# The experts' stage: VectorE makes all parts of the low weights, GpSimd only moves rows

## The reference, cut to what matters

```
for e in range(16):
    hid = silu(xt @ exp_w1[e]) * (xt @ exp_w3[e])        # 1024 -> 256, twice
    y   = y + gate[:, e:e+1] * (hid @ exp_w2[e])         # 256 -> 1024
```

## Time and profile before

| | us |
|---|---|
| median of 3 runs (lowest to highest) | 1619.41 (1618.01 to 1620.03) |
| the profiled execution | 1620.24 |
| its span in the profile | 1618.5 |
| experts: first up_lo on VectorE to the last y_ps matmul | 1126.6 to 1550.3 |
| TensorE busy in the span | 1449.3 (90%) |
| VectorE busy in the span | 1125.9 (70%) |
| GpSimd busy in the span | 483.4 (30%) |

### The profile page before, as it was taken

One profiled execution on the slowest core, in us unless ns is written; L12 is line 12 of the kernel. 1 busy time (PEld: TensorE's weight loads), 2 busy tenths in 40 slices (PEclk: granted clock), 3 DMA queues, 4 the chain that ended last, 5 costly groups with the idle time before them and its releaser, 6 DMA issues. The chain is left out here.

```text
span 1618.5 us, 30220 instructions
## 1 busy us (share of the span) xinstructions
PE 1449.3 (90%) x8946; PEld 1261.0 (78%) x8947; DVE 1125.9 (70%) x2208; ACT 927.7 (57%) x1625; POOL 483.4 (30%) x345
## 2 busy tenths in 40 slices
PE   5999989999976899999999999973999999999940
PEld 5999977777754899999999999972777788777820
DVE  8787548999955888888888888877444333444237
ACT  3444338787855766666666666632555544556325
POOL 1212124575520011111121111122454534544218
PEclk9999999999988999999999999995899999999975
DMA  8865542534444112211112221126798787796576
GB/s 286 303 226 200 211 145 86 189 144 173 165 147 138 61 39 93 72 65 59 59 60 80 76 78 59 47 97 198 233 270 263 182 248 207 200 273 164 104 224 257
DMA packets 126214, 250.09 MB, mean 155 GB/s; under 512 B 24498, under 2 KB 77746, under 8 KB 126132
## 3 DMA queue, kind: packets, MB, share of 16 engines
q1 hardware_dynamic: 94000, 160.97, 28.7%
q0 software_dynamic: 12528, 45.99, 12.3%
q10 hardware_dynamic: 19604, 42.09, 6.8%
HBM read 154.35 MB, written 94.67 MB: 154 GB/s over the span
## 5 line engine op out<-in xcount | busy, mean ns | idle before, releaser
L1736 DVE TENSOR_TENSOR d_probs_t_lo<-d_pt_ps,d_probs_t_hi 128x512 fp32r<-128x512 f32 x256 | 164.9, 686 | 63.4 <-ACT d_probs_t_hi L1650 61.8
L1914 POOL TENSOR_TENSOR d_h_tile<-d_s_tile,d_ln_g_b 128x512 f32<-128x512 f32 x30 | 38.9, 1296 | 532.3 <-ACT d_s_tile L1683 514.6
L1650 ACT ACTIVATE d_probs_t_hi<-d_pt_ps 128x512 fp32r<-128x512 f32 x256 | 139.2, 596 | 95.9 <-PE d_pt_ps L1531 89.5
L1712 DVE TENSOR_REDUCE d_neg_max<-d_s_ps 128x1 f32<-128x1024 f32 x128 | 155.6, 1215 | 3.5 <-PE d_s_ps L1520 3.5
L121 PE MATMUL acc<-k_hi,wl_hi 128*128 128x256 f32 x512 | 145.2, 284 | 4.5 <-DVE k_lo L576 4.5
L121 PE MATMUL e_a_ps<-up_hi,e_xt_hi 128*128 x336 | 136.6, 406 | 10.8 <-issue 5.5
L1633 ACT ACTIVATE d_probs<-d_s_ps,d_neg_max 128x1024 f32<-128x1024 f32 x128 | 143.5, 1121 | 4.2 <-DVE d_neg_max L1712 4.2
L122 PE MATMUL acc<-k_lo,wl_hi 128*128 128x256 f32 x512 | 144.3, 282 | 0.0
L123 PE MATMUL acc<-k_hi,wl_lo 128*128 128x256 f32 x512 | 144.3, 282 | 0.0
L1531 PE MATMUL d_pt_ps<-ident,d_probs 128*128 128x128 f32 x1024 | 132.9, 273 | 4.7 <-ACT d_probs L1633 3.2
L1545 PE MATMUL d_ot_ps<-d_probs_t_hi,d_v_split 128*128 128x256 f32 x512 | 127.4, 287 | 8.3 <-DVE d_probs_t_lo L1736 8.3
(11 more groups left out here) (405 smaller groups left out, 4079.2 us busy)
## 6 DMA issues: line engine op xcount, KB each, us to landing
up_raw<-in_exp_w SPq DMA_DIRECT2D x32, 1024.0 KB, 13.0
down_raw<-in_exp_w SPq DMA_DIRECT2D x16, 1024.0 KB, 13.0
d_h_tile<-h_dram SPq DMA_DIRECT2D x16, 522.0 KB, 4.7
h_dram<-v_all ACTq DMA_DIRECT2D x16, 512.0 KB
ht_hi_dram<-k_hi ACTq DMA_DIRECT2D x8, 1024.0 KB, 4.3
ht_lo_dram<-k_lo ACTq DMA_DIRECT2D x8, 1024.0 KB, 6.7
q_dram<-wq_raw ACTq DMA_DIRECT2D x16, 512.0 KB, 3.0
d_q_tile<-q_dram SPq DMA_DIRECT2D x16, 512.0 KB, 4.2
```

The lines of the kernel that those rows point to most:

```text
L1650: act.activation(pt_hi[:, c * HALF:(c + 1) * HALF, h % 2], pt_ps[c][:], ACT.Copy).then_inc(pth_done[c], 1)
L1712: dve.tensor_reduce(nm[:, u, h:h + 1], s_ps[h % 2][:], AX, ALU.max, negate=True).then_inc(nm_done, 1)
L1736: dve.tensor_tensor(pt_lo[:, part, h % 2], pt_ps[c][:], pt_hi[:, part, h % 2].bitcast(F32), ALU.subtract)\
L1914: pool.tensor_tensor(h1[:, part], s_t[u][:, part], g_b[:, part], ALU.mult).then_inc(hg_done, 1)
```

## The change

GpSimd makes no low weights any more. VectorE makes all four up parts in `split_first` and both down parts in `split_rest`. The two semaphores of GpSimd go, and every consumer waits for four up parts and two down parts of VectorE alone. The same holds before the first tile. Buffers, matmuls, transfers and ScalarE's work are as they were.

```diff
-        UP_POOL = 3
-        DOWN_POOL = 1
...
-        up_lo_pool = sem("up_lo_made_by_pool")
-        down_lo_pool = sem("down_lo_made_by_pool")
...
-        up_lo_parts = ((up_lo_made, UP_PARTS - 1), (up_lo_pool, 1))
-        down_lo_parts = ((down_lo_made, DOWN_PARTS - 1), (down_lo_pool, 1))
+        up_lo_parts = ((up_lo_made, UP_PARTS),)
+        down_lo_parts = ((down_lo_made, DOWN_PARTS),)
...
         def _(pool):
...
-            def split_rest(e):
-                make_up_lo(pool, e, UP_POOL, up_lo_pool)
-                make_down_lo(pool, e, DOWN_POOL, down_lo_pool)
...
-            split_rest(0)
-            last = run_tiles(pool, skip, ahead, None, skip, skip, down, skip, split_rest)
+            last = run_tiles(pool, skip, ahead, None, skip, skip, down, skip, None)
...
         def _(dve):
...
             def split_first(e):
                 for i in range(UP_PARTS):
-                    if i != UP_POOL:
-                        make_up_lo(dve, e, i, up_lo_made)
+                    make_up_lo(dve, e, i, up_lo_made)
 
             def split_rest(e):
                 for k in range(DOWN_PARTS):
-                    if k != DOWN_POOL:
-                        make_down_lo(dve, e, k, down_lo_made)
+                    make_down_lo(dve, e, k, down_lo_made)
```

## The result

The changed kernel takes 1644.71 us (median of 4 runs, 1638.77 to 1647.53) against 1619.72 us for the kernel before (4 runs beside them, 1618.01 to 1623.37). The ratio is 1.0129, 95% interval 1.0106 to 1.0152: slower, by 17 to 25 us (the two medians alone lie 25.0 us apart, at the top of that). The forecast was 1634.8 us, in a range of 1628 to 1643. By the ratio, 1.0129 x 1619.41 = 1640.3 us, the result lies near the upper end of that range; the median itself lies above it. The direction and the main term were right, and some 8 us are missing.

A forecast was written before the change was run, and what follows sets the result against it. TensorE sets the pace and loses time in split tiles, where `hid` stands behind VectorE's up parts. 16.0 - 0.3 - 0.3 = +15.4 us gave 1634.8 us on the runs' median, range 1628 to 1643.

The forecast's parts named there:

- the main term: In 14 split tiles, a fourth VectorE up part makes `hid` and TensorE 1.14 us later each: 16.0 us.
- The fourth up part: In split tiles, one more subtraction ahead of `hid` delays TensorE 1.14 us in each of 14 tiles: 16.0 us.
- The distance behind hid: Between the end of `hid` and the next tile, what TensorE does doesn't change; 1.27, 2.15 or 2.56 us.
- Weight loads and scatters: Earlier loads delay scatters before seven split tiles, 0 to +8.4 us; longer experts gain 0 to -4; both taken as 0.
- The second down part: In plain tiles, VectorE's second down part ends before `hid` is due, with over 1 us slack behind it: 0 us.
- GpSimd's leaving: TensorE's wait for GpSimd before tile 4 goes, -0.3 us; tile 4's high parts wait less for SP, -0.3 us.
- Tile 0 and the rest: Extra subtractions before tile 0 are hidden and its block's earlier start covers 1.14 us: 0 us; stages outside experts don't move.
- signs of being wrong: Wrong if `hid` idles before it in split tiles, plain tiles grow, split blocks start elsewhere, or stages outside experts move.
- late scatters: Rival, 10%: before seven split tiles each `gate` is the whole 1.2 us late, 8.4 us more, 1643 us.
- GpSimd is what TensorE waits for: Rival, 3%: each change of expert hangs on GpSimd's up part; 0.6 us won at 14 changes, 1611 us.
- nothing moves: Rival, 4%: `hid` late by 1.14 us is absorbed somewhere behind TensorE's matmuls, 1619 us.

The follow-up runs named there:

- repeat1: Kernel before, with VectorE repeating one up subtraction into an unread spare buffer behind its three up parts, ahead of `hid`; ratio 1.0124 to the kernel before.
- up_only: Changed kernel without its second half: VectorE makes all four up parts, GpSimd keeps down part 1; ratio 1.0123 to the kernel before.
- gate_late: Kernel before, with VectorE copying `gate` and scatter indices of the previous tile right behind `hid` of the next; 1616.70 us, ratio 0.9956 to the kernel before.
- change_gate_late: Changed kernel, with VectorE copying `gate` and scatter indices of the previous tile behind `hid` of the next; 1629.48 us, ratio 1.0038 to the kernel before.
- repeat2: Kernel before, with VectorE repeating one up subtraction twice into unread spare buffers ahead of `hid` in split tiles; ratio 1.0321 to the kernel before.
- down_wait: down_only, but GpSimd begins its up part only when VectorE's two down parts are done; ratio 1.0002 to the kernel before.
- down_only: Changed kernel without its first half: VectorE makes both down parts, GpSimd keeps up part 3; ratio 1.0089 to the kernel before.
- pool_late1: Kernel before, GpSimd keeping its two parts, with VectorE's third up part moved behind `hid` into the next tile; ratio 1.0011 to the kernel before.

## Why the prediction was right, and what it missed

**The fourth up part, +16.0: right.** Four in a row take 4.63 us, `hid` follows without a gap, and tiles such as 21 grow by 1.06. repeat1 shows that an extra subtraction ahead of `hid` is enough: without any other part of the change it gives the same time, by these 16.0 us and two terms that came with it in both kernels, late blocks and the clock.

**The distance behind hid: missed, -1.3.** The prediction said that what TensorE does between two tiles doesn't change. It has one wait less there: about 0.1 us in each of 14 tiles, as up_only shows too.

**Weight loads and scatters, taken as 0: this step failed in its sign and place.** The prediction weighed a loss of up to 8.4 us in the seven split tiles behind experts of two tiles, and a gain of up to 4 us behind the long ones. It went the other way round. Behind the short experts next to nothing was late (tiles 4 and 28 began their block earlier, tiles 8 and 26 0.1 to 0.2 us later). Behind the long ones, in tiles 11, 17, 24 and 33, the scatter landed late (waits of 1.42, 1.00, 1.20 and 1.23 us) and the block started 0.6 to 1.3 us later: +2.5 net, or +3.6 without tile 4, which is GpSimd's (below). That the wait for the scatter is what this costs, gate_late and change_gate_late show. That an earlier load makes the scatter late, as the prediction had it for the short experts, no run shows, and it isn't needed: in repeat1 the load is closer to the scatter than before in tiles 11, 24 and 33, and the waits are there too (0.68, 0.64 and 1.02 us). What does make it late stays open. A load in flight may have a part in it: over the ten traces without the late gate, `gate` waits for a landing in 44 of the 50 cases of tiles 11, 14, 17, 24 and 33, with a load asked for 9 to 17 us before the tile, and in none of tiles 21 and 35, with the last one 18 us or more before. No run took the load away.

**The clock: a term that was missing, +5.6.** All idle time was priced at its own length. In the kernel before that held, since no tile from 2 on was followed by a half-clock stretch. At 2.7 to 4.2 us of idleness in a tile (33, 11 and 24) it does not: tiles 12, 25 and 34 pay 7.0 us (and tile 1, by chance of that one execution, 1.4 less). A price taken from 14 tiles that are each a little late was carried over to tiles that are later than any of them. This term also differs from run to run: of the changed kernel's four runs the fastest (1638.77 us) has a granted clock of 0.955 over its whole span, the others (1643.53 to 1647.53) 0.949 to 0.951. That the clock follows the idle time is read from the traces (last section) and fits repeat2, whose stretches grew from five to eleven.

**The second down part, 0: right, for this change.** down_wait shows it. But down_only shows what the prediction didn't see: with GpSimd still subtracting it would have cost 14 us. The bounds given for it were worked out from rows in which VectorE always came first.

**GpSimd's leaving, -0.6: too small.** Tile 3 is 0.3 us shorter, and would be more but for a slow read of the flag. In tile 4 ScalarE no longer waits 3.82 us for SP but 2.46 ("issue"), and the block starts 1.08 us earlier, where the prediction took 0.3 of at most 1.4. Together -1.4. The slow reads, +1.3, were not foreseen; plain tiles were expected at 9.33. What makes them slow stays open: in the changed kernel they come 0.1 to 1.7 us behind the issue of a weight load, but gate_late has eight of 0.56 to 1.19 us with none issued near.

**Tile 0 and the rest: right**, within 0.3 us.

Together: +16.0 - 1.3 + 2.5 + 5.6 + 1.3 - 0.3 = +23.8 against +23.7 in the trace and +15.4 forecast. By the prediction's own signs of being wrong, two came true: the plain tiles grew, and in four split tiles the block starts later than before, one of them 14.0 us long. That the total still lies in the range by the ratio is in part luck, as the clock was not in the sum and the late scatters stood in it at 0. Of the rivals, late scatters had a part in it, at less than half of the 8.4 us and in other tiles. "GpSimd is what TensorE waits for" is refuted by repeat1, and "nothing moves" by all of it.

## What to carry to other kernels

Before work is moved from an engine that is seldom busy to a fast one, look at what stands behind it in the fast one's queue: here 1.22 us put ahead of the instruction that TensorE waits for cost 20 us, and the same put behind it cost 6, or nothing once a wait that stood in the same queue was moved too. When a cost is extrapolated from short idle times of TensorE, ask whether some will grow to a length behind which the traces show the granted clock at half; here that took up to 7 us more. And when VectorE and GpSimd both subtract from SBUF, the pair should be ordered on purpose, as a trace in which one always comes first doesn't show what happens when it doesn't.

## What the hardware did that was not expected

- Half clock behind idle TensorE. Over ten traces (before, after, and the eight kernels from up_only to pool_late1), by TensorE's idle time in a tile from 2 to 40, a stretch at the 1.2 GHz level followed none of the 321 tile ends with under 1.5 us of idleness, 9 of the 37 with 1.5 to 2.5 us, and 27 of the 32 with 2.5 us or more.
- VectorE and GpSimd block each other in both directions: VectorE's subtraction of 1.22 us took 3.42 and up to 6.20 us behind GpSimd's, and GpSimd's, at best 2.35 us, up to 3.39 where VectorE's ran beside it.
- A scatter's instruction on GpSimd took 2.37 to 2.64 us instead of 1.59 in 9 cases after the change and 2 before, when a subtraction of VectorE had begun 0.05 to 0.32 us earlier.
- TensorE's sequencer reads a flag in 0.30 us, and in some plain tiles behind a split one in 0.56 to 1.64 us; the slow reads looked at (in gate_late and the changed kernel) came 3.0 to 4.7 us behind the start of a scatter's instruction, but so did some fast ones.
